# Attention: reciprocal sums applied by GpSimd, transposition banks emptied by ScalarE, differential values paired

## The reference

```python
p = softmax(q @ k * scale)            # A, B, D: the sink is in A's sum; o = p @ v
out = o[:, :, :, 0] - lam * o[:, :, :, 1]      # C: two softmaxes over the same values
out = rmsnorm(out, subln) * (1 - lam_init)     # over each head's 64 columns
```

## Time and profile before

| | us |
|---|---|
| median of 3 runs | 2220.06 |
| lowest, highest | 2217.28, 2224.57 |
| the profiled execution | 2215.74 |
| its span | 2213.9 |
| TensorE busy | 2000.4 (90%) |
| VectorE busy | 713.4 (32%) |
| ScalarE busy | 512.4 (23%) |
| GpSimd busy | 157.1 (7%) |

### The profile page before, as it was taken

One profiled execution on the slowest core, in us unless ns is written; L12 is line 12 of the kernel. 1 busy time (PEld: TensorE's weight loads), 2 busy tenths in 40 slices (PEclk: granted clock), 3 DMA queues, 4 the chain that ended last, 5 costly groups with the idle time before them and its releaser, 6 DMA issues. The chain is left out here.

```text
span 2213.9 us, 27681 instructions
## 1 busy us (share of the span) xinstructions
PE 2000.4 (90%) x10862; PEld 955.0 (43%) x10862; DVE 713.4 (32%) x1825; ACT 512.4 (23%) x1212; POOL 157.1 (7%) x155
## 2 busy tenths in 40 slices
PE   5999988999988999999999899889998698888875
PEld 3445454555543332323323556456555233333322
DVE  3322345666552100101001632366655202020203
ACT  3211144554441010100100421254444100000001
POOL 1101100000001001020100201000000000000000
PEclk9999979999999999999999999999999899999999
DMA  9832110000078999999999302100005999999995
GB/s 343 305 136 75 24 53 1 1 2 1 1 287 364 422 374 408 400 373 426 364 410 423 144 20 76 41 37 1 1 1 218 370 427 426 427 427 426 427 426 230
DMA packets 90938, 515.69 MB, mean 233 GB/s; under 512 B 10594, under 2 KB 15628, under 8 KB 36540
## 3 DMA queue, kind: packets, MB, share of 16 engines
q1 hardware_dynamic: 84496, 493.29, 54.9%
q0 software_dynamic: 4416, 15.21, 2.3%
q10 hardware_dynamic: 1900, 5.43, 0.6%
HBM read 498.69 MB, written 15.20 MB: 232 GB/s over the span
## 5 line engine op out<-in xcount | busy, mean ns | idle before, releaser
L702 PE MATMUL psS<-arena 128*64 128x512 f32 (+9 forms) x4552 | 1139.1, 557 | 66.4 <-DMA arena<-in_w_up 24.1
L702 PEld LDWEIGHTS psS<-arena 128*64 128x64 f32 (+4 forms) x4552 | 452.5, 159 | 663.1 <-issue 591.7
L705 PE MATMUL psT<-ident,arena 128*128 128x128 f32 (+1 forms) x1036 | 170.4, 287 | 79.1 <-DVE arena L1923 21.0
L1909 DVE TENSOR_REDUCE mx<-psS 128x1 f32<-128x768 f32 (+2 forms) x200 | 165.4, 827 | 160.3 <-PE psS L702 157.1
L1266 ACT ACTIVATE arena<-psT 128x512 f32<-128x512 f32 (+5 forms) x265 | 130.2, 493 | 304.8 <-PE psT L705 291.9
L2092 DVE TENSOR_TENSOR arena<-arena,psS 128x512 f32<-128x512 f32 x32 | 20.6, 684 | 549.4 <-PE psS L702 549.4
L1266 ACT ACTIVATE arena<-psS 128x128 f32<-128x128 f32 (+5 forms) x158 | 61.8, 421 | 571.7 <-PE psS L702 526.3
L705 PEld LDWEIGHTS psT<-ident,arena 128*128 128x128 f32 (+1 forms) x1036 | 117.5, 143 | 171.7 <-issue 110.1
L702 PE MATMUL psT<-arena 128*32 128x512 f32 x1536 | 174.5, 595 | 0.0
L1266 ACT ACTIVATE arena<-psS,nb 128x768 f32<-128x768 f32 (+2 forms) x200 | 158.6, 794 | 14.6 <-DVE nb L1914 13.0
L702 PE MATMUL psO<-arena 128*64 128x128 f32 (+2 forms) x1600 | 149.4, 293 | 0.0
(11 more groups left out here) (228 smaller groups left out, 1330.9 us busy)
## 6 DMA issues: line engine op xcount, KB each, us to landing
arena<-in_w_gate SPq DMA_DIRECT2D x117, 1024.0 KB, 17.4
arena<-in_w_up SPq DMA_DIRECT2D x116, 1024.0 KB, 18.8
arena<-in_w_down SPq DMA_DIRECT2D x116, 1024.0 KB, 25.9
arena<-in_w_mod SPq DMA_DIRECT2D x48, 1024.0 KB, 7.5
arena<-in_w_in SPq DMA_DIRECT2D x6, 2048.0 KB, 7.8
arena<-in_w_out SPq DMA_DIRECT2D x8, 512.0 KB, 7.8
arena<-in_w_out SPq DMA_DIRECT2D x2, 2048.0 KB, 15.9
normed_rows<-arena ACTq DMA_DIRECT2D x8, 512.0 KB, 8.1
```

The costliest lines, as they stand in the source:

```text
L702: return nc.tensor.matmul(o, lhsT, rhs, start=start, stop=stop)
L705: return nc.tensor.transpose(o, in_, ident[0:n, 0:n])
L1909: link(V.reduce_max(mx[:, par:par + 1], view(S, 0, P, 0, (512, 2), (1, n)), axis=AX.XY))
```

## The change

- The reciprocal of every A, B and D unit's sum is taken for itself, at its `ahead` place on VectorE (with the sink's addition for A). GpSimd then multiplies that unit's probabilities in place in SBUF (`divided`), and TensorE waits for that (semaphore dv) before it transposes them.
- TensorE's spreads and VectorE's multiplications of L1959 go. ScalarE's copy of psO is the result.
- ScalarE copies all of psT, VectorE none. PTd goes.
- C's values are computed like the others': two units at the odd one, transposed. ScalarE copies them out, TensorE transposes them back at the step where pv is unit 12, and VectorE multiplies those by reciprocals into OS. `norm_steps` is one step later, T_AT two steps later, Q_AT of A, B0 and B1 one earlier.
- Pieces of the output projection come before the turns of a step.

The diff without the list of semaphores (PTd out; dv and Cf in):

```diff
--- before.py
+++ after.py
@@ -54,9 +54,9 @@
 VCOL = [0] * 4 + [128, 128, 256, 256] + [384, 384, 512, 512] + [640] * 4
 LAG = 2
 
-T_AT = 0
+T_AT = 2
 Q_PARTS = ("A", "B0", "B1", "D", "C1")
-Q_AT = {5: "A", 6: "B0", 7: "B1", 12: "D", 13: "C1"}
+Q_AT = {4: "A", 5: "B0", 6: "B1", 12: "D", 13: "C1"}
 O_COUNT = {3: 2, 4: 2, 5: 2, 6: 2, 8: 2, 9: 2, 10: 2, 11: 2}
 assert sum(O_COUNT.values()) == 2 * KD
 
@@ -149,7 +149,7 @@
 
 def norm_steps(plan):
 
-    return {n: entry[2] // TURNS for n, entry in enumerate(plan) if entry[2] is not None and entry[2] % TURNS == 11}
+    return {n: entry[2] // TURNS for n, entry in enumerate(plan) if entry[2] is not None and entry[2] % TURNS == 12}
 
 
 def uses_act(sec, t):
@@ -400,7 +400,7 @@
         Z = [sems(l, "sq xn ht htev htevd proj pact pdve dsq bsq bt btev bs bsa bsd kn kpe kt "
                      "P O mj me gp ge ce") for l in range(L)]
 
...
         for z in Z:
             z.update(once)
 
@@ -429,7 +429,11 @@
 
         def shared_groups(l, i, g):
 
-            return 3 * (l * TT + i) + (0, 1, None, 2)[g] + 1
+            return 4 * (l * TT + i) + g + 1
+
+        def divisions(l, i, u):
+
+            return 12 * (l * TT + i) + (u if u < 8 else u - 4) + 1
 
         def exchanged_through(l, i, n):
 
@@ -631,21 +635,35 @@
                 z = Z[l]
                 powers(PAIRS + 2 * TT)
 
-                def exchanged(i):
-
-                    for n, name in enumerate(("A", "D", "C1")):
-                        pool.wait_ge(z["me"], turns_through(PLANS[l], ("Q", i, name)))
-                        a = QT + (i % 2 * QTILES + Q_PLACE[name]) * P
-                        nc.gpsimd.tensor_copy(ar[64:128, a + 256:a + 512], ar[0:64, a:a + 256]).then_inc(z["qs"], 1)
-                        pool.wait_ge(z["qs"], exchanged_through(l, i, n) - 1)
-                        nc.gpsimd.tensor_copy(ar[0:64, a + 256:a + 512], ar[64:128, a:a + 256]).then_inc(z["qs"], 1)
-                        pool.wait_ge(z["qs"], exchanged_through(l, i, n))
-
-                exchanged(0)
-                for i in range(len(TILES[l])):
-                    if i + 1 < len(TILES[l]):
-                        exchanged(i + 1)
-                    powers(1)
+                def exchanged(i, name):
+
+                    n = ("A", "D", "C1").index(name)
+                    pool.wait_ge(z["me"], turns_through(PLANS[l], ("Q", i, name)))
+                    a = QT + (i % 2 * QTILES + Q_PLACE[name]) * P
+                    nc.gpsimd.tensor_copy(ar[64:128, a + 256:a + 512], ar[0:64, a:a + 256]).then_inc(z["qs"], 1)
+                    pool.wait_ge(z["qs"], exchanged_through(l, i, n) - 1)
+                    nc.gpsimd.tensor_copy(ar[0:64, a + 256:a + 512], ar[64:128, a:a + 256]).then_inc(z["qs"], 1)
+                    pool.wait_ge(z["qs"], exchanged_through(l, i, n))
+
+                def divided(i, u):
+
+                    slot = LAST_SLOT[u]
+                    j, par = i * SLOTS + slot, i % 2 * SLOTS + slot
+                    a, n = PB + j % 4 * NTOK, 2 * half_width(TILES[l][i], slot)
+                    pool.wait_ge(z["rr"], divisions(l, i, u))
+                    nc.gpsimd.tensor_scalar(ar[:, a:a + n], ar[:, a:a + n], rr[:, par:par + 1], None, ALU.mult).then_inc(z["dv"], 1)
+                    pool.wait_ge(z["dv"], divisions(l, i, u))
+
+                for name in ("A", "D", "C1"):
+                    exchanged(0, name)
+                for step, (s, v, pv, turns, pieces, ahead) in enumerate(PLANS[l]):
+                    if ahead is not None and not 8 <= ahead % TURNS < 12:
+                        divided(*divmod(ahead, TURNS))
+                    for kind, i, name in turns:
+                        if kind == "Q" and name in ("A", "D", "C1"):
+                            exchanged(i, name)
+                    if step in norm_steps(PLANS[l]):
+                        powers(1)
                 powers(2)
 
                 nx, F = SW[l] // P, FP[l]
@@ -800,7 +818,7 @@
                         b, col = 5, 256
                         pe.wait_ge(z["me"], n - 1)
                         if values is not None:
-                            pe.wait_ge(z["PTd"], l * TT * TURNS + values + 1)
+                            pe.wait_ge(z["PTa"], l * TT * TURNS + values + 1)
                     if kind == "T":
                         pe.wait_ge(z["Cn"], l * TT + i + 1)
                         for c in range(2):
@@ -1035,10 +1053,9 @@
                             pe.wait_ge(z["mixed"], (l * TT + i) * 4 + u - 7)
                             s0 -= 1
                         else:
-                            pe.wait_ge(z["P"], s0 + 1)
+                            pe.wait_ge(z["dv"], divisions(l, i, u))
                         if v:
                             pe.wait_ge(z["PTa"], l * TT * TURNS + v)
-                            pe.wait_ge(z["PTd"], l * TT * TURNS + v)
                             jobs = [x for p in PLANS[l][:step] for x in p[3]]
                             if jobs:
                                 pe.wait_ge(z["me"], turns_through(PLANS[l], jobs[-1]))
@@ -1051,32 +1068,26 @@
                     if pv is not None:
                         i, u = divmod(pv, TURNS)
                         pe.wait_ge(z["PTa"], l * TT * TURNS + pv + 1)
-                        pe.wait_ge(z["PTd"], l * TT * TURNS + pv + 1)
                         kt = [k for k, _ in places_of(tiles[i], LAST_SLOT[u])]
-                        if pv >= 4 and (u % 4 == 0 if 8 <= u < 12 else u % 4 == 1):
-                            pe.wait_ge(z["Og"], 4 * (l * TT + i) + u // 4)
-                        if 8 <= u < 12:
-                            for n, k in enumerate(kt):
-                                a, b = PT[pv % 3] + n * P, VV + k * 768 + VCOL[u]
-                                last = mm(psO[:, u % 4 * P:(u % 4 + 1) * P], ar[:, a:a + P], ar[:, b:b + P], n == 0, n == len(kt) - 1)
-                            last.then_inc(z["O"], 1)
-                        elif u % 2:
+                        if pv >= 4 and u % 4 == 1:
+                            pe.wait_ge(z["Og"], shared_groups(l, i, u // 4) - 1)
+                        if u % 2:
                             for n, k in enumerate(kt):
                                 for h in range(2):
                                     a, b = PT[(pv - 1 + h) % 3] + n * P, VV + k * 768 + VCOL[u] + 64 * h
                                     last = mm(psO[64 * h:64 * h + 64, u % 4 // 2 * P:(u % 4 // 2 + 1) * P], ar[:, b:b + 64],
                                               ar[:, a:a + P], n == 0, n == len(kt) - 1)
                             last.then_inc(z["O"], 2)
-                        if u % 4 == 2 and u // 4 != 2:
-                            pe.wait_ge(z["rr"], shared_groups(l, i, u // 4))
-                            for n in range(4):
-                                r0 = i % 2 * SLOTS + LAST_SLOT[u - 2] + n
-                                mm(psO[n % 2 * 64:n % 2 * 64 + 64, (2 + n // 2) * P:(3 + n // 2) * P],
-                                          view(rr, 0, P, r0, (0, 64)), ident[:, :])
+                        elif u == 12:
+                            pe.wait_ge(z["Oc"], l * TT + i + 1)
+                            for c in range(2):
+                                a = QN + tiles[i] * QNW + (4 + c) * P
+                                last = tr(psO[:, (2 + c) * P:(3 + c) * P], ar[:, a:a + P])
+                            last.then_inc(z["Cf"], 1)
+                    for x in pieces:
+                        output_piece(*x)
                     for x in turns:
                         turn(*x, values=v)
-                    for x in pieces:
-                        output_piece(*x)
                     if step in TAIL:
                         n = TAIL[step]
                         if n == 0:
@@ -1469,7 +1480,7 @@
                         act.wait_ge(z["T"], l * TT * TURNS + v + 1)
                         if v >= 3:
                             act.wait_ge(z["O"], v - 2)
-                        w = min(len(keys_of(tiles[i], LAST_SLOT[u])), 4) * P
+                        w = len(keys_of(tiles[i], LAST_SLOT[u])) * P
                         a = PT[v % 3]
                         a_(ar[:, a:a + w], psT[:, 0:w]).then_inc(z["PTa"], 1)
                     for slot in UNIT_SLOTS[s % TURNS] if s is not None else ():
@@ -1492,11 +1503,11 @@
                         for g in range(4):
                             act.wait_ge(z["gt"], 4 * l + g + 1)
                             a_(gate(g), bank(4 + g)).then_inc(z["gtev"], 1)
-                    if pv is not None and pv % 4 == 3 and pv % TURNS // 4 != 2:
+                    if pv is not None and pv % 4 == 3:
                         i, u = divmod(pv, TURNS)
                         act.wait_ge(z["O"], pv + 1)
                         o = QN + tiles[i] * QNW + u // 4 * 2 * P
-                        a_(ar[:, o:o + 256], bank(6, w=256)).then_inc(z["Oc"], 1)
```

(44 more changed lines are left out.)

## The result

The changed kernel takes 2268.57 us (2265.95 to 2272.04), the kernel before 2219.57 in the same sessions: a ratio of 1.0219, 95% interval 1.0203 to 1.0235. 2208 was forecast, 2194 to 2226 as the range. Its profiled execution took 2267.98 us (span 2266.2), 52 more than that of before.

What follows compares the result with a forecast made beforehand. TensorE, busy 59.67 of 64.74 us a latent tile, was taken to bound only where nothing else is nearly as late. Seven tiles at 0.8 (5.6) plus context 6.1, taken as 12, off the 2220.06 median: 2208, range 2194 to 2226.

Steps and rivals of the forecast that it cites:

- The price of the multiply: GpSimd's 128x768 multiply in SBUF, twelve a tile: 0.85 us taken, upper bound 1.64, plus 0.1 each way for semaphores.
- the walk's own slope: At six tile boundaries, multiply time above 0.85 us counts three times: hold of VectorE's square, hold of its normalising, T(0).
- The walk: Step-by-step timing of a latent tile from step 11 to the next: 63.9 us instead of 64.73, 0.8 of 4.3 gained.
- layer 1's first tile: Latent tile without output-projection pieces, taken as bound by the C loop already: gain 0.
- the tails: After the last scores, bound by power, reciprocal, GpSimd and T(15), the turning of unit 15's probabilities: within 0.3 of before.
- slower: GpSimd becomes the bound at the boundary: Rival, step 15 to step 3: +2 at a 1.64 us multiply, +14 (2234) at 2.3 us; chance 0.14.
- The clock: Rival: less busy TensorE in latent tiles gets granted clock 0.94, losing 10 of 12 us: 2218; chance 0.13.
- The context tiles: Two tiles before the latent ones: 2.2 and 1.5 from shorter boundary chains, 0.9 and 1.5 from spreads and C values, together 6.1.
- Step 7: Stays bound by its exponential in a latent tile, the two emptyings in its way being longer: +0.2 us.
- The C loop: Scores, two maxima, two exponentials, scores, where TensorE waits on ScalarE: 4.27 us becomes 4.5, step 9's removed spread not gained.
- The pause before the C1 turn: Step 13: T(11) ends at 9.35, and the C1 query turn then waits for ScalarE's emptying until 10.25.
- The collision: VectorE instructions with two SBUF inputs wait out GpSimd's whole remaining operation; without this, each full tile 0.7 us shorter.

Runs made afterwards that it cites:

- e11_fill7: e5_fill with two more 512-column matmuls on TensorE in step 7 behind T(5), the turning of unit 5's probabilities: 2248.66 us, ratio 1.0132.
- e5_fill: Changed kernel with added 512-column matmuls filling TensorE's pauses, one at step 0 and three at step 2 of every tile but a layer's first: 2256.01 us.
- e8_pairs: e4_spread with VectorE's share of the emptying back, leaving C's paired values and the moved steps: 2216.97 us, ratio 0.9988.
- e7_evac: Kernel before with one part of the change, ScalarE emptying all columns of the transposition banks and VectorE none: 2225.36 us, ratio 1.0023.
- e6_fill8: e1_narrow8 with two 512-column matmuls added on TensorE at step 2: 2210.84 us, ratio 0.9952.
- e1_narrow8: Changed kernel with GpSimd's twelve multiplies a tile cut to 8 columns, the rest left undivided: 2216.44 us, ratio 0.9983.
- e4_spread: Changed kernel with the normalising of before (four reciprocals at once, TensorE's spreads, VectorE's product) and no GpSimd multiply: 2213.50 us, ratio 0.9969.
- e10_turn14: e4_spread with the C1 query turn moved from step 13 to step 14: 2197.49 us, ratio 0.9894.

## Why the prediction was wrong

- **The price of the multiply** is the step that failed first. It was put at 0.85 us, from a copy's start and a memset's slope, with 1.64 as the upper bound; it takes 2.205 us. Neither row held the operation: a copy moves a value, the power row has 8 columns and says nothing of a slope. The true price lies outside the bounds, so the range could not hold. By the walk's own slope (18 us for each us) the excess of 1.35 us is 24: a forecast of 2232.
- **The slope** failed next, though not inside a latent tile. The walk at the true price gives 63.9 + 3 x 1.35 = 67.95 us, and e11_fill7, with the clock at 1.00, has 67.40. That this fits is in part luck. Two of the walk's three places are VectorE held by the multiply, and that hold is 0.35 us at the square and none at the normalising (last section). In their place T(14), T(15), T(2), T(6) and T(12) wait for GpSimd (T(14) 0.56 and T(15) 1.34 in e5_fill, the last three 0.69, 0.22 and 0.38 in the changed kernel). Left out of the sum were the clock, layer 1's first tile, put at 0 (from its C scores to the next tile's 62.74 us before, 70.71 after), and the tails, put within 0.3: in layer 0's, T(14) and T(15) wait 2.66 and 1.69 us for GpSimd, where before had one wait of 2.03. Above the knee the slope of the whole is 43. The rival "slower: GpSimd becomes the bound at the boundary" had mechanism, engine and place right and gave +14 for 2.3 us, where +49 came.
- **The clock** was a rival at 0.13 and a loss of 10 us. Its kind was right: 0.95 in the latent tile at 85% busy. It is no alternative to the others but comes with them, and filling three pauses returned 20 us. The busy share of a tile, by which the prediction went, does not tell it: 90% in e8_pairs at 1.00 (57.57 of 63.88), 93% in e7_evac at 0.95 (62.57 of 67.25).
- **The context tiles** were to give 6.1 us. Together they give nothing. From the first context tile's C scores to the second's took 42.85 us before and 46.00 in e8_pairs, which has no multiply of GpSimd's; the clock there fell from 0.80 to 0.70, as the two lines (before, then e8_pairs) show. With as many records TensorE is busy 4.5 us longer and idle 1.4 us less, so the loss is in the slower clock. Why it fell is not shown; that the shorter value products left TensorE emptier is an argument. The next stretch, from the second context tile to the first latent one, gained 1.6 (53.10 to 51.50).

```profile
293.94:336.79 42.85, 35.14 (x229) 22.65 (x229) 20.94 (x71) 19.59 (x70) 4.01 (x7) 0.80 0.00 1
```

```profile
296.99:342.99 46.00, 39.65 (x230) 23.59 (x231) 20.95 (x71) 20.07 (x70) 4.01 (x7) 0.70 0.00 1
```

- **What held.** The walk in a latent tile, once price and clock are put in: 62.25 for 62.41 measured in e6_fill8. TensorE's work in it: 57.41 us there less 1.9 for the two added matmuls is 55.5, where 55.4 was forecast. Step 7, 3.84 before (450.78 to 454.62) and 0.2 more by the walk: 3.98 (523.52 to 527.50 in e1_narrow8). The C loop at 4.5 (467.57 to 471.96 there, 4.39). ScalarE's 768 columns in 0.81. The pause before the C1 turn. That only part of what is taken off TensorE comes through: e8_pairs, which has 2.5 of the 4.3 us, is 0.8 us shorter than before at full clock. It can be more where stalls go as well: 2.2 in e4_spread and 3.1 in e10_turn14.
- **The collision** was too dear in one direction and is not exclusive, as below.

## What to carry to other kernels

A price for an operation that the trace lacks is the largest risk of a sum: where the nearest rows do other work, give the bound room by the operation's kind, and see what the sum becomes at twice the guess. Work taken from the busiest engine is worth only what no other chain takes up, and a pause on TensorE can be paid twice, once as itself and once in the matmuls behind it; a few useless matmuls in the pause tell the two apart. Executions of one kernel can differ in this (by 14 us in e4_spread), so one profiled tile is read with its clock beside it and not alone. An operation put into a chain costs little while other waits cover it: here 12 us for each us up to 1.25 us, and 43 beyond.

## What the runs showed of the hardware

GpSimd's multiply by a per-partition factor costs 2.5 ns a column, VectorE's 0.62 us in all for 768. Work of VectorE beside it is held, but not to its end. In the changed kernel (GpSimd, then VectorE):

```profile
501.85 2.20 POOL L654 TENSOR_SCALAR arena<-arena,rr 128x768 f32<-128x768 f32 x1 [1.35 <-DVE rr L1944]
```

```profile
502.25 0.77 DVE L1888 TENSOR_TENSOR arena<-arena 128x256 f32<-128x256 f32 x1
...
507.31 0.42 DVE L1895 TENSOR_TENSOR arena<-arena,pwr 128x256 f32<-128x256 f32 x1
```

The square with two SBUF inputs starts 0.40 us into the multiply and takes 0.77 instead of 0.42, ending a whole microsecond before the multiply does. Over the ten tiles it takes 0.70 on average, and 0.43 in e4_spread, where GpSimd has no multiply. The product of 507.31, also with two SBUF inputs, runs beside the next multiply (506.33 to 508.57) and takes its usual 0.42. The Trainium skill, SBUF: State Buffer, "Who interferes with whom", calls the ports that the two engines share an exclusive lock, for which a VectorE instruction with two SBUF inputs contends with a GpSimd instruction that reads SBUF. Read as a lock for the whole of the earlier instruction, that would have held the square to 504.05. Here the measurement decides: the hold was 0.35 us.
